# Seven block products for a second feed-forward's middle input group, and where the modulation tiles then go

## The reference, cut to what matters

```python
def swiglu(h, w_in, w_out):                      # w_in 1024 x 5632, w_out 2816 x 1024
    g, u = jnp.split(h @ w_in, 2, axis=-1)
    return (jax.nn.silu(g) * u) @ w_out

def ffn_sublayer(x, g, shift, scale, gate, w_in, w_out):
    return x + FFN_RES * gate * swiglu(modulate(rms_norm(x, g), shift, scale), w_in, w_out)

mx = jnp.split((silu_c @ w_mod[i] + b_mod[i])[:, None, :], N_MOD, axis=-1)   # shift, scale, gate of
mc = jnp.split((silu_cc @ w_mod[i] + b_mod[i])[None, None, :], N_MOD, axis=-1)   # three sub-layers
```

## Time and profile before

| what | value |
|---|---|
| device time, median of 3 (range) | 1629.0 us (1626.96 to 1629.19) |
| the profiled execution: its own time | 1628.09 us |
| its span, first to last instruction | 1626.3 us |
| mean granted TensorE clock | 0.994 |
| PE busy | 1604.1 us |
| DVE busy | 1238.0 us |
| ACT busy | 654.7 us |
| POOL busy | 227.5 us |

### The profile page before, as it was taken

How to read it: one execution, slowest core, us unless ns; L and a number is a source line. 1 busy time by engine, 2 the same in 40 slices (tenths; PEclk the granted TensorE clock), 3 DMA queues, 4 the chain that set the end, 5 groups by cost and what they waited for, 6 DMA issues and landing times.

```text
span 1626.3 us, 25014 instructions
## 1 busy us (share of the span) xinstructions
PE 1604.1 (99%) x9558; PEld 1410.7 (87%) x9558; DVE 1238.0 (76%) x2024; ACT 654.7 (40%) x935; POOL 227.5 (14%) x160
## 2 busy tenths in 40 slices
PE   9999999999999999999999999999999999999998
PEld 6788888889877798888889998899989998999997
DVE  5878888778488679878888688787647787666665
ACT  3321221224688532212235443245335456543433
POOL 0000000000598100000034000044133021000000
PEclk8999999999999999999999999999999999999999
DMA  8755655543211226655547436357456332155552
GB/s 328 279 193 184 220 211 203 192 168 106 102 53 52 77 107 245 220 199 190 208 115 187 148 124 239 136 135 181 139 125 170 110 130 71 59 185 191 194 193 78
DMA packets 56813, 262.25 MB, mean 161 GB/s; under 512 B 6432, under 2 KB 6560, under 8 KB 39072
## 3 DMA queue, kind: packets, MB, share of 16 engines
q1 hardware_dynamic: 50976, 250.75, 43.4%
q0 software_dynamic: 5760, 10.49, 3.9%
HBM read 249.68 MB, written 1.05 MB: 154 GB/s over the span
## 4 chain that ended last, share of the span: by engine, by line
PE 86%; DVE 5%; POOL 3%; ACT 2%; issue 2%; DMA 2%; SPq 0%; DVEq 0%; ACTq 0%; POOLq 0%
PE ps L2233 11%; PE ps L2035 10%; PE ps L2036 10%; PE ps L2037 10%; PE ps L2199 9%; PE ps L2200 9%; PE ps L2206 9%; PE ps L2764 5%; PE ps L2062 4%; PE ps L2770 2%; POOL spare L688 2%; PE ps L2383 1%; PE ps L2295 1%; DVE w_lo L1455 1%; PE ps L2679 1%
## 5 line engine op out<-in xcount | busy, mean ns | idle before, releaser
L2199 PE MATMUL ps<-a_hi,w_hi 128*128 128x512 f32 x640 | 249.3, 390 | 0.9 <-ACT w_hi L926 0.9
L2200 PE MATMUL ps<-a_lo,w_hi 128*128 128x512 f32 x640 | 249.0, 389 | 0.0
L2035 PE MATMUL ps<-h_hi,w_lo 128*128 128x512 f32 (+1 forms) x648 | 235.0, 363 | 0.1
L2036 PE MATMUL ps<-h_lo,w_hi 128*128 128x512 f32 (+1 forms) x648 | 233.4, 360 | 0.0
L2037 PE MATMUL ps<-h_hi,w_hi 128*128 128x512 f32 (+1 forms) x648 | 233.4, 360 | 0.0
L1455 DVE TENSOR_TENSOR w_lo<-raw,w_hi 128x2048 fp32r<-128x2048 f32 x89 | 203.5, 2286 | 22.1 <-ACT w_hi L761 13.2
L1261 DVE CUSTOM_DVE_ANT_0 mring<-mring,cb 128x1024 f32<-128x1024 f32 x128 | 156.2, 1220 | 0.0
L1259 DVE CUSTOM_DVE_ANT_0 unread<-mring,cb 128x1024 bf16<-128x1024 f32 x128 | 156.0, 1219 | 0.1
L2206 PE MATMUL ps<-a_hi,w_lo 128*128 128x512 f32 x640 | 151.6, 389 | 0.0
L2199 PEld LDWEIGHTS ps<-a_hi,w_hi 128*128 128x128 f32 x640 | 120.1, 188 | 26.5 <-issue 0.9
L2206 PEld LDWEIGHTS ps<-a_hi,w_lo 128*128 128x128 f32 x640 | 120.1, 188 | 24.9
(11 more groups left out here) (403 smaller groups left out, 3471.2 us busy)
## 6 DMA issues: line engine op xcount, KB each, us to landing
raw<-wstream SPq DMA_DIRECT2D x126, 1024.0 KB, 5.0
mring<-wmod SPq DMA_DIRECT2D x144, 512.0 KB, 3.6
spare<-wstream SPq DMA_DIRECT2D x11, 1024.0 KB, 4.8
extra<-wstream SPq DMA_DIRECT2D x20, 512.0 KB, 4.1
raw<-wstream SPq DMA_DIRECT2D x20, 512.0 KB, 5.3
raw<-wstream SPq DMA_DIRECT2D x20, 256.0 KB, 5.3
extra<-extra POOLq DMA_DIRECT2D x20, 256.0 KB, 3.4
raw<-raw POOLq DMA_DIRECT2D x20, 256.0 KB, 4.5
```

Of the source, the lines that this page charges most:

```text
L2035: pe.matmul(dst, lhs_lo, rhs_hi, start=start, stop=False, skip_group_check=True)
L2036: pe.matmul(dst, lhs_hi, rhs_lo, start=False, stop=False, skip_group_check=True)
L2199: pe.matmul(bank, hi, a_hi[:, k, 0:nt], start=k == 0, stop=False, skip_group_check=True)
L2200: pe.matmul(bank, hi, a_lo[:, k, 0:nt], start=False, stop=False, skip_group_check=True)
```

## The change

1. Group 1 of the second feed-forward is fast: `FAST` is ((), (1, 2), (1, 2), ()), which makes 28 fast slabs. Its token sums are now made before group 1.
2. The tiles: the first feed-forward takes 72 (three for each output slab behind group 0, and 3, 2, 3, 3, 2, 3 in group 2), the second 28 and the third 28. In the second and the third, 20 stand in group 0 and 8 are "late": 3, 3, 2, 0 with the four output slabs between groups 1 and 2.
3. The late tiles are loaded into `sq`, `ss` and the two halves of `work`, buffers that fast steps use. SP loads the first three when the last product of group 1 is made, the fourth when its low part is made; ACT's fast group begins with a wait for all of them. On SP's queue these loads stand among the slab loads and ahead of the next fast slabs' quarter loads (`late_mods`).
4. In `fast_step` on DVE, `part_low(1)` moves from ahead of line 1511 to behind it.
5. `finalize` (1, 1) moves to behind group 0 of the third feed-forward, (1, 2) to behind its group 2.

```diff
-MOD_COUNTS = (((2,) * 8, (2,) * 4, (2, 3) * 4, (2,) * 4, (2,) * 6), ((2, 3) * 4, (2,) * 4, (2, 3) * 4, (), ()),
-              ((2,) * 8, (), (), (), ()), ((),) * 5)
+MOD_COUNTS = (((2,) * 8, (3,) * 4, (2, 3) * 4, (2,) * 4, (3, 2, 3) * 2), ((2, 3) * 4, (), (), (3, 3, 2, 0), ()),
+              ((2, 3) * 4, (), (), (3, 3, 2, 0), ()), ((),) * 5)
-FAST = ((), (2,), (1, 2), ())
+FAST = ((), (1, 2), (1, 2), ())
+        mod_slots = tuple(mring[:, c] for c in range(4))
+        late_slots = tuple(x.rearrange("p a n -> p (a n)") for x in (sq[:], ss[:], work[:, 0:2], work[:, 2:4]))
...
             # SP
+            def late_mods(w, f, n):
+                plain(w, w + 3)
+                sp.wait_ge(pair_free, f + 2)
+                for k in range(3):
+                    mod_tile(n + k, (n + k) % 4, n + k - 3, late_slots)
+                sp.wait_ge(hid_ready, f)
+                mod_tile(n + 3, (n + 3) % 4, n, late_slots)
+                plain(w + 3, w + 4)
+                for k in range(4, 7):
+                    mod_tile(n + k, (n + k) % 4, n + k - 3, late_slots)
+                quarter_loads(w + 4, w % 2, w + 3)
+                mod_tile(n + 7, (n + 7) % 4, n + 4, late_slots)
+                quarter_loads(w + 5, (w + 1) % 2, w + 4)
...
+            for s in (1, 2):
+                w, f, counts = FFN_W[s], s * FFN_STEPS + GROUPS[0] + GROUPS[1], MOD_COUNTS[s][0]
+                if s == 2:
+                    sp.wait_ge(slab_done, W_FFN2 - 4)
+                for k in range(4):
+                    mod_tile(n + k, k, n + k - 3)
+                stepped(w + 4, n + 4, counts, n + sum(counts))
+                n += sum(counts)
+                fast_loads(w + 12, GROUPS[1])
+                late_mods(w + 20, f, n)
+                n += sum(MOD_COUNTS[s][3])
+                fast_loads(w + 26, GROUPS[2] - 2)
+                w1 = w + 30
+                if s == 1:
+                    plain(w1, W_FFN2 + 4)
...
             # ACT
-            def fast_group(w, f, n, size):
+            def fast_group(w, f, n, size, dots):
+                act.wait_ge(mod_dots, dots)
...
             # DVE, fast_step
                 if ahead:
                     part_low(0, n + 1, w + 1, 1 - p, i)
-                    part_low(1, n + 1, w + 1, 1 - p, i)
                 else:
                     turn_low(w + 1, slice(0, 3 * QUARTER))
                 product(4)
                 earlier(2)
                 dve.tensor_tensor(up_sum[:, LAT:TOK], neg_u3, ps[GATE2_BANK[p]][:, 0:LAT],
                                   ALU.subtract).then_inc(combined, 1)
+                if ahead:
+                    part_low(1, n + 1, w + 1, 1 - p, i)
                 product(5)
...
             # DVE, the output slabs ahead of a fast group
+                        n, late = FAST_BASE[s, g + 1], list(MOD_COUNTS[s][phase]) or [0] * 4
                         for j in range(2):
-                            out_tiles(sub, b, w, j, nt)
+                            out_tiles(sub, b, w, j, nt, None, (0,))
+                            if j == 0 and late[0]:
+                                mod_dots_at(n0, 1, None, late_slots)
+                            out_tiles(sub, b, w, j, nt, None, (1,))
                             split_lo(w + j + 2, (w + j) % 2)
                             if first:
                                 token_sums(j, T_USE[s])
+                            if late[j]:
+                                done = 1 if j == 0 else 0
+                                mod_dots_at(n0 + done, late[j] - done, None, late_slots)
+                            n0 += late[j]
                         out_tiles(sub, b, w, 2, nt)
...
                         part_low(1, n, w + 4, 0)
+                        if late[2]:
+                            mod_dots_at(n0, late[2], None, late_slots)
+                        n0 += late[2]
                         out_tiles(sub, b, w, 3, nt)
...
-            n0 = ffn(1, TOK, lambda s, w, b: both_tail(s, "ffn2", w, b), n0, ((), (1, 0), (1, 1)))
-            n0 = ffn(2, TOK, lambda s, w, b: both_tail(s, "mla", w, b), n0, ((), (1, 2)))
+            n0 = ffn(1, TOK, lambda s, w, b: both_tail(s, "ffn2", w, b), n0, ((), (1, 0)))
+            n0 = ffn(2, TOK, lambda s, w, b: both_tail(s, "mla", w, b), n0, ((1, 1), (), (1, 2)))
```

More of the change, by code:

```diff
@@ L437, in part_source, with mods_done @@
                     raw[:, p, 2 * QUARTER:SLAB])[part]
+        def mods_done(s, phase):
+            return MOD_FIRST + sum(sum(x) for stage in MOD_COUNTS[:s] for x in stage) + \
+                sum(sum(x) for x in MOD_COUNTS[s][:phase])
         def value_at(i, factor, const):
@@ L558, in slab, with mod_tile @@
                   .then_inc(raw_loaded[slot], 16)
[L560 removed]
+            def mod_tile(n, slot, wait=None, slots=mod_slots):
                 if wait is not None:
                     sp.wait_ge(mod_dots, wait)
[L563 removed]
+                sp.dma_start(slots[slot], wmod[ds(n, 1)].rearrange("a p n -> p (a n)")) \
                   .then_inc(mod_loaded[slot], 16)
@@ new lines, in _ @@
+            n, counts = MOD_FIRST, [c for phase in MOD_COUNTS[0] for c in phase]
+            stepped(W_FFN0 + 4, n + 4, counts, n + sum(counts))
+            plain(W_FFN0 + 4 + len(counts), W_FFN1 + 4)
+            n += sum(counts)
[6 more added lines that the diff above has]
+                stepped(w + 4, n + 4, counts, n + sum(counts))
+                n += sum(counts)
+                fast_loads(w + 12, GROUPS[1])
[5 more added lines that the diff above has]
+                    plain(w1, W_FFN2 + 4)
@@ L1432, in lat_tail, with out_tiles @@
                     split_lo(w + 5, (w + 1) % 2)
-            def out_tiles(s, b, w, j, nt, i=None):
+            def out_tiles(s, b, w, j, nt, i=None, tiles=(0, 1)):
                 k = (lambda x: x) if i is None else (lambda x: i + x)
-                for t in range(2):
+                for t in tiles:
                     dve.wait_ge(*((slab_done, k(w + j + 1)) if t else (tile0_done, k(b + j + 1))))
@@ L1638, in ffn @@
                         continue
-                    with dve.Fori(0, 3, 2) as i:
-                        for j in range(2):
-                            out_tiles(sub, b, w, j, nt, i)
-                            split_lo(w + j + 2, (w + j) % 2, i)
-                            if MOD_COUNTS[s][phase]:
-                                mod_dots_at(n0 + 2 * j, 2, i)
-                    n0 += sum(MOD_COUNTS[s][phase])
+                    if 3 in MOD_COUNTS[s][phase]:
+                        for j, dots in enumerate(MOD_COUNTS[s][phase]):
+                            out_tiles(sub, b, w, j, nt)
+                            split_lo(w + j + 2, (w + j) % 2)
+                            mod_dots_at(n0, dots)
+                            n0 += dots
+                    else:
+                        with dve.Fori(0, 3, 2) as i:
+                            for j in range(2):
+                                out_tiles(sub, b, w, j, nt, i)
+                                split_lo(w + j + 2, (w + j) % 2, i)
+                                if MOD_COUNTS[s][phase]:
+                                    mod_dots_at(n0 + 2 * j, 2, i)
+                        n0 += sum(MOD_COUNTS[s][phase])
                     phase += 1
```

38 lines of the change are left out of this document (6 added, 32 removed).

## The result

The kernel with the change takes 1632.5 us (median of 8 runs, 1630.54 to 1636.09), against 1628.4 for the kernel before (8 runs, 1626.96 to 1629.60). The ratio is 1.0024, interval 1.0014 to 1.0033: slower by 0.24%, where 1621.0 was predicted and a gain had been given 91 in 100. The profiled execution took 1630.66 us, with a span of 1628.9, so 2.6 us more than the span before.

The account below looks back on a forecast made before the run. PE, busy 99% of the span, was taken to bound the kernel. Slabs -6.5, slips -1.1 and 0 for tiles, sums and late loads made -7.6 us, so 1621.0 us; 8-in-10 range 1618.0 to 1624.5.

Parts of the forecast that it names:

- The slabs: Second feed-forward's group 1: eight slabs made fast, 10.07 us each in place of 10.88, -6.5 us in all.
- The spacing by the Trainium skill: Rival, chance 0.03: new fast slabs run at the page's matmul spacing, 10.6 us less, 1618.4.
- The slips: Third feed-forward's middle group: two pace slips go once part_low(1) stands behind the third combination, -1.1 us.
- the added group: Second feed-forward's new fast group: its quarter loads, accumulating DMAs and POOL sums stay covered, 0; bound another 1.1 us.
- The tiles in the first feed-forward: Eight more tiles there fit into DVE's idle time and the tail, 0; upper bound 2.3 us.
- The late tiles' dots, and the loads that they hold: Between groups 1 and 2 of both stages: DVE has room, quarter loads leave 6.5 us late but covered, 0.
- hidden by 4 us: Start of group 2: ACT's new wait for the dots precedes the first evictions, due about 1.5 us in; no cost.
- 3.4 + 1.3: POOL's accumulating DMA and sum for the first fast slab of group 2: from 1188.5, done at 1193.2.
- 8.7 us are left: Slack from POOL's first sum, after ACT's and DVE's work, to PE's first use of its part at 1204.7.
- 2.5 us left: DVE's slack before group 2: done at about 1200.8, while the last output updates can't start before 1203.28.
- Slower: Rival, chance 0.04: late quarter loads and stretched POOL sums delay PE 10.8 us at each of two boundaries, +14, 1643.
- 12.5 us: Load delay, instead of 6.5, at which PE would wait over 3.8 us at each boundary and the sign turn.

Follow-up runs that it names:

- e6: The kernel before with only the move of part_low(1) behind line 1511; 1627.6 us, ratio 0.9994.
- e5: The change without late tiles and with part_low(1) back ahead of line 1511, so the fast groups alone; 1621.5 us, ratio 0.9958.
- e4: The change without late tiles: the first feed-forward takes 88 tiles, the second and third 20 each in group 0; 1621.1 us, ratio 0.9959.
- e3: The change with the last two late tiles' dots on DVE ahead of the first fast slab's low parts 0 and 1; 1622.4 us, ratio 0.9970.
- e2: The change with SP holding the eighth late tile and second fast slab's quarter loads until POOL's first three-block sum is made; 1620.55 us, ratio 0.9953.
- e10: e4's kernel with the second slab's quarter loads of group 2 leaving when the first slab's have landed, as POOL's accumulating DMA starts; 1626.7 us, ratio 0.9994.
- e8: e4's kernel with the first fast slab's quarter loads of group 2 held one split longer, to leave with the second slab's; 1622.9 us, ratio 0.9962.
- e7: The change with part_low(1) back ahead of line 1511; 1633.6 us, ratio 1.0035.

## Why the prediction was wrong

**The slabs, -6.5: right.** Eight fast slabs take 80.52 us, 10.07 apart, as the earlier trace rows had them. The spacing by the Trainium skill (TensorE: Matmul & The Clock Gate, Back-to-back issue gap), 9.17 us a slab as an estimate, was rightly not used: the page gives that formula for an isolated matmul and says that in a stream the weight loads count too, and 10.07 us for 84 matmuls, each with its weight load, is again 119.8 ns.

**The slips, -1.1: right in the trace, not shown by runs.** Group 1 of the third is 80.58 us long, the slips are gone in e6's trace too, and one comes back in e5's, without the move; but the times of e4 and e5, and of e6 and the kernel before, show no difference that can be told. That the added group has no slips of its own (0) was right.

**The tiles in the first feed-forward, 0: right.** The second feed-forward's first read comes at 605.07, against 605.03 before, and e4, with 24 tiles more there than before, is as quick as the forecast.

**The late tiles' dots, and the loads that they hold: right up to POOL's first sum.** The first slab's quarter loads left later as said: 820.23, with group 2 at 842.35, is 22.1 us ahead of the group, where it was 28.2 before, so 6.1 late for the 6.5 forecast. ACT's new wait for the dots was forecast to be hidden by 4 us. It was not: the dots themselves came late, and ACT's first eviction stood 2.2 us behind them, in the third 1.5 us. PE's wait ended later still, on DVE's part 2 at 850.4, so no cost of its own shows.

```profile
846.57 0.38 ACT L858 ACTIVATE sq<-ps 128x256 f32<-128x256 f32 x1 [2.21 <-DVE stage L1280]
```

**"3.4 + 1.3", the accumulating DMA and the sum: this is the step that failed.** The 3.4 us was read in a place where the next load was issued 2.0 us later (1099.67 and 1101.68 in the trace of the kernel before). The prediction itself had put the two events on each other: "8.7 us are left" rests on POOL taking up at "about 1188.5", and two sentences earlier the second slab's loads leave at "1188.5 instead of 1185.9". (By its own 6.1 us between load and POOL the first would have been 1187.6; the trace has 7.3 us between them.) In the kernel before, POOL took up 4.7 us ahead of those loads. The measured times are 1187.18 and 1187.22, in a trace in which this group starts 1.2 us earlier than before, and from issue to sum it took 8.8 us: some 5 us of them behind the loads' packets. I moved a transfer and kept its duration from the place it came from.

**"8.7 us are left", the slack: wrong by what it counted.** It counted until PE needs the part that the sum makes. This part was still in time: DVE had it at 840.7, ahead of the group's start at 842.35. But the instruction waiting for it holds DVE's queue, and behind it stood 4 dots of 1.2 us, the updates, and parts 2 and 3. For these the slack was the other number, "2.5 us left". 5.1 us of idle, 2.0 us by which POOL's sums stretched a dot and a copy (2.31 for 1.22, 1.07 for 0.17) and the 2.5 us of slack make 4.6 us; the updates were 5.2 us late. e3 shows this half alone: with the dots ahead of the wait, the same slow DMA leaves PE without a wait in both groups 2, and the ratio is 0.9970, not told apart from e4's 0.9959, where the change has 1.0024.

**The clock: not in the prediction.** The lower level added 1.7 us to each boundary, some 3.4 of the 10.3 us given back.

**The rivals.** "Slower", given 4 in 100, had the right place and the right queue, and the right turning point in PE's time: over 3.8 us at each boundary, where it was 6.4 and 3.9. The delay that it named for it, 12.5 us, was a wrong sum: 8.7 us was what is left after the 6.5 us, so 3.8 us of waiting needed 6.5 + 8.7 + 3.8 = 19.0 us. (The stretched sum of four "near 1202" is 1203.1 by the prediction's own terms, 1193.2 + 4.3 + 1.3 + 4.3; nothing hangs on it.) Of its two delays the first (6.1 us) was real and by itself harmless, as e2 shows, which keeps it. The second, dots that stretch POOL's sums, was there in a small way and in both directions: beside dots sums took 1.9 to 2.4 us, not 5.6, and the dots were stretched too. The rule on DVE and GpSimd in the Trainium skill (SBUF — State Buffer, SBUF: two separate sides) fits both; it is not what decided. What decided, a transfer that stands behind others, was in none of the cases. "Nothing in the rows makes it so large" was said of rows none of which had both transfers in one instant.

**What stays open.** That POOL's transfer stood behind the loads' packets is in the traces, and that it does so only where loads are issued beside it is shown by e2 and e10. Why a load issued 0.03 to 0.42 us behind it still goes ahead of it, and one 1.2 us behind does not, and what sets that order, is not. The spread is open too. The runs of the change have a median 1.8 us above the profiled one. That the coincidence, at the edge of a few tenths of a us, falls out differently from run to run is argued from the spread of e10 and e3 beside that of e2, and not shown: e2 has only four runs, e6, the kernel before with one line moved, spreads over 5.7 us, and only one execution of each kernel was profiled. The clock does not explain e10's spread: its run of 1628.0 us had the highest mean granted clock of the eight, 0.996, and that of 1621.2 had 0.994.

## What to carry to other kernels

When a step moves a transfer, list what else is issued in the instant to which it goes, and price it there: a duration read elsewhere is that of another neighbourhood. Slack behind a wait in a queue in order is the smallest over everything behind the waiting instruction, and not that of the result it waits for. Where two transfers meet, holding the less urgent one until the urgent one has landed can be one wait on an existing semaphore: here it turned +0.24% into -0.47%.

## What the runs showed of the hardware

- An accumulating DMA within SBUF of 256 KB (issue to the waiting sum) takes 3.4 to 3.7 us in nearly all places, 8.2 to 9.0 when a slab's quarter loads (1.25 MB) are issued in the same instant, within 0.3 us, and 4.3 to 4.6 when the last of 2.5 MB of loads was issued some 4 us earlier (e8). Its first packet moves 1.4 to 1.6 us behind the issue in the common case, and 4.2 to 5.8 us behind it in the slow one, when only the loads' packets have moved. The two views of the transfer from issue to landing, the changed kernel in 826 to 838 us, and e2 in 827 to 842:

```profile
extra<-extra POOLq DMA_DIRECT2D x1, 256.0 KB, 8.5
```

```profile
extra<-extra POOLq DMA_DIRECT2D x1, 256.0 KB, 3.4
```

- In the changed kernel a PE wait of 2.9 us, and one of 2.2 us, was each followed by some 3.4 us at the lower clock level (1.2 GHz), which cost another 1.7 us; one of 1.5 us was not. The length of the wait alone does not decide it: in e7 one of 2.6 us (to 851.4) was followed by a granted clock of 1.00, and one of 1.8 us (in 1212 to 1215) by 0.57 and 0.86 over 3 us each.
- DVE's dot with two SBUF inputs took 2.3 us in place of 1.22 when a POOL sum ran beside it, and a copy of 128 x 8 values 1.07 us in place of 0.17.
